# A filter's spectra from folded time rows: 34 DFT blocks in place of 58, a rounded two-pass filter product, and the token projections dealt out among the rounds

## The reference

```python
def hyena_filter_spectra(L, w_in, w_hid, b, freq, w_out):      # L = 1024
    t = jnp.linspace(0.0, 1.0, L)[:, None]
    ...
    for k, w in enumerate((w_in, w_hid[0], w_hid[1])):          # hidden width 64
        hdn = jnp.sin(freq[k] * (hdn @ w + b[k]))
    h = (hdn @ w_out).reshape(L, HY_ORDER, 2, HY_WIDTH)         # (1024, 2, 2, 1024)
    h = h * jnp.exp(-t * deltas)[:, None, None, :]
    hf, hb = h[:, :, 0], h[:, :, 1]
    k_circ = jnp.concatenate([hf[:1] + hb[:1], hf[1:], jnp.zeros_like(hf[:1]), hb[:0:-1]], axis=0)
    return jnp.fft.rfft(k_circ, axis=0)                         # length 2048
```

```python
def rms_norm(x, g):
    return (x * lax.rsqrt(jnp.mean(jnp.square(x), axis=-1, keepdims=True) + EPS) * g)
```

## Time and profile before

| | before |
|---|---|
| time, median of 3 runs | 3007.36 us (3007.21 to 3008.28) |
| span of the profiled execution | 3007.8 us |
| PE busy over the span | 2735.8 us (91%) |
| DVE busy | 1814.4 us (60%) |
| ACT busy | 919.7 us (31%) |
| POOL busy | 864.6 us (29%) |

### The profile page before, as it was taken

The page is one execution under the profiler, slowest core; times in us unless marked ns, Lnnn a source line. Parts: engine busy times, 40 slices in busy tenths (PEclk is TensorE's granted clock), DMA queues, the critical chain, the costliest instruction groups (busy, mean ns, idle before and its releaser), DMA issues. The chain is left out here.

```text
span 3007.8 us, 30927 instructions
## 1 busy us (share of the span) xinstructions
PE 2735.8 (91%) x11377; PEld 1868.0 (62%) x11377; DVE 1814.4 (60%) x2979; ACT 919.7 (31%) x1668; POOL 864.6 (29%) x635
## 2 busy tenths in 40 slices
PE   7999989978679978789999999996999997999967
PEld 3544444547546556577787899985778885444456
DVE  6255229999577658765841555553774424888553
ACT  2111121100334332536434566553432220111132
POOL 0000000005022137576633233325642221343235
PEclk9999999989889989999999999998999998999979
DMA  4211411110100034244756323314421123111043
GB/s 152 81 70 60 144 65 42 31 47 1 57 1 1 1 147 153 65 147 159 272 177 212 94 46 92 75 31 150 137 85 42 49 72 142 60 60 60 28 172 108
DMA packets 109562, 269.80 MB, mean 90 GB/s; under 512 B 18464, under 2 KB 34664, under 8 KB 105001
## 3 DMA queue, kind: packets, MB, share of 16 engines
q1 hardware_dynamic: 109418, 267.90, 26.7%
HBM read 206.87 MB, written 60.99 MB: 89 GB/s over the span
## 5 line engine op out<-in xcount | busy, mean ns | idle before, releaser
L313 PE MATMUL psum<-part,part 128*128 128x512 f32 (+1 forms) x1984 | 766.8, 386 | 78.0 <-POOL part L1604 28.1
L314 PE MATMUL psum<-part,part 128*128 128x512 f32 (+1 forms) x1984 | 743.2, 375 | 0.0
L315 PE MATMUL psum<-part,part 128*128 128x512 f32 (+1 forms) x1984 | 741.6, 374 | 0.0
L1604 POOL TENSOR_TENSOR part<-arena,part 128x512 fp32r<-128x512 f32 (+1 forms) x298 | 426.0, 1440 | 633.0 <-ACT part L1598 632.7
L313 PEld LDWEIGHTS psum<-part,part 128*128 128x128 f32 x1984 | 379.2, 191 | 163.8 <-POOL part L1604 68.5
L314 PEld LDWEIGHTS psum<-part,part 128*128 128x128 f32 x1984 | 380.2, 192 | 70.9 <-issue 3.2
L315 PEld LDWEIGHTS psum<-part,part 128*128 128x128 f32 x1984 | 378.8, 191 | 72.4
L1598 ACT ACTIVATE part<-arena 128x512 fp32r<-128x512 f32 (+1 forms) x298 | 181.6, 620 | 364.8 <-PE psum L315 237.5
L221 PE MATMUL psum<-arena 128*128 128x512 f32 (+1 forms) x672 | 232.3, 505 | 17.4 <-DMA arena<-in_w_f 9.7
L1135 POOL TENSOR_TENSOR arena<-arena 128x256 f32<-128x256 f32 x56 | 39.1, 700 | 704.7 <-PE psum L1148 704.7
L766 PE MATMUL psum<-arena 128*128 128x512 f32 x464 | 200.6, 593 | 0.7 <-issue 0.7
(11 more groups left out here) (311 smaller groups left out, 4003.8 us busy)
## 6 DMA issues: line engine op xcount, KB each, us to landing
arena<-in_ada_w SPq DMA_DIRECT2D x24, 1024.0 KB, 5.5
arena<-in_w_hy SPq DMA_DIRECT2D x40, 512.0 KB, 3.3
scratch_spec<-arena SPq DMA_DIRECT2D x68, 256.0 KB, 2.0
arena<-scratch_spec SPq DMA_DIRECT2D x12, 1024.0 KB, 5.1
arena<-in_w_gate SPq DMA_DIRECT2D x16, 512.0 KB, 3.9
arena<-in_w_out SPq DMA_DIRECT2D x16, 512.0 KB, 3.8
arena<-in_w_mgate SPq DMA_DIRECT2D x16, 512.0 KB, 3.7
arena<-in_w_mout SPq DMA_DIRECT2D x16, 512.0 KB, 4.2
```

Source lines behind the costliest of these rows:

```text
L313: nc.tensor.matmul(acc, a_hi, b_hi, start=start, stop=False)
L314: nc.tensor.matmul(acc, a_hi, b_lo, start=False, stop=False)
L315: return nc.tensor.matmul(acc, a_lo, b_hi, start=False, stop=stop)
L1604: self.K.nc.gpsimd.tensor_tensor(self.lo[s][:, c], self.raw[s][:, c], self.hi[s][:, c].bitcast(F32), ALU.subtract).then_inc(self.split, 1)
```

## The change

Every stage but the first has the same instructions as before. In `stage_spectra_tokens`:

- **Time order.** The host lays the 1024 times out as 512 early ones and, beside each t, its mirror 1024 - t. `fold_even` adds and subtracts the two halves (two operations of 2048 elements), so that every block of frequencies needs 128 rows of cosine and 128 of sine: two matmuls for each, 34 in a pair of s, 136 in all. `fold_odd` does the turns for the odd residues. Both work on `ed` and `Y`, of which there is now one each, not one for each s.
- **Product.** The hidden output and the output weights are split into a rounded part and a rest. `hid` has 128 rows: the rounded part in rows 0 to 63, the rest in 64 to 127 (layer 2 of the hidden layers is computed twice, in both halves of the rows). The product is two matmuls on rounded operands (L820 and L821 in the kernel after) for each tile. DVE takes two tiles at a time out of PSUM.
- **Order.** Eight rounds k, one for each half, order and s. Each has an even part (residues 0, 4, 2 and 6, with 10 matmuls for s = 0 and 8 for s = 1) and an odd part (8 matmuls). The products of round k + 1 stand before and between the two parts of round k, the tokens of one tile at the start of rounds 0 to 6 and of one more in the middle of rounds 0 and 1. ACT computes the decay for 512 channels at a time. Two PSUM banks serve the blocks, not four, and one each the latents and the values, not two.
- **Transfers.** The tokens are loaded in three pieces of columns straight to where the next stage wants them; before, they were loaded in this stage and again at its end (L555).

```diff
 def spec_blocks(n, comp):
-    size = lambda m: len(RES_TILES[min(PAIRS[m], 8 - PAIRS[m])])
...
+    at = 2 if comp == 2 else NSPEC0 + 2 * n if comp == 1 else 2 * n + 2 if n else 0
+    return [(at + q, y) for q, y in enumerate(SPEC_SLOTS[PAIRS[n]])]
-def radix(K, dve, link, x, Y, tmp, ready):
...
+def fold_even(K, dve, link, x, sums, Y, s, ready):
+    v = K.nc.vector
+    early, late = x[:, 0:4, :], x[:, 4:8, :]
+    v.tensor_tensor(sums, early, late, ALU.add)
+    link(v.tensor_tensor(early, early, late, ALU.subtract))
+    even, odd = (sums, early) if s == 0 else (early, sums)
+    v.tensor_tensor(Y[:, 0:2, :], even[:, 2:4, :], even[:, 0:2, :], ALU.add)
+    link(v.tensor_tensor(Y[:, 2:4, :], even[:, 2:4, :], even[:, 0:2, :], ALU.subtract))
+    dve.sem_inc(ready, 1)
+    if s == 0:
+        v.tensor_copy(even[0:1, 2, :], odd[0:1, 2, :])
+        link(v.tensor_tensor(odd[0:1, 2, :], odd[0:1, 2, :], x[0:1, 6, :], ALU.add))
+    ends, turned = even[:, 0:4:2, :], Y[:, 1:4:2, :]
+    v.scalar_tensor_tensor(out=Y[:, 4:6, :], in0=turned, scalar=C8, in1=ends, op0=ALU.mult, op1=ALU.add)
+    link(v.scalar_tensor_tensor(out=Y[:, 6:8, :], in0=turned, scalar=-C8, in1=ends, op0=ALU.mult, op1=ALU.add))
+    dve.sem_inc(ready, 1)
+    return odd
+def fold_odd(K, dve, link, x, odd, Y, s, ready):
...
+    if s == 1:
+        link(K.nc.vector.tensor_copy(Y[0:1, 12:16, :], x[0:1, 6, :].unsqueeze(1).broadcast_to((1, 4, HALF))))
...
@@ vector @@
             make_weights()
...
+            rest_of_weights(0)
+            for j in range(2):
+                cols = slice(j * HALF, (j + 1) * HALF)
+                dve.wait_ge(hid_rounded, j + 1)
+                v.tensor_tensor(hid[64:128, cols], h_raw[64:128, cols], hid[64:128, cols].bitcast(F32), ALU.subtract)\
+                    .then_inc(hid_split, 1)
+            for k, (o, h, s) in enumerate(ORDER):
+                dve.wait_ge(decay_ready, h + 1)
+                for q in range(4):
...
+                    v.tensor_tensor(ed[:, 2 * q:2 * q + 2, :], acc, decay[:, 2 * q:2 * q + 2, :], ALU.mult)\
+                        .then_inc(hd_ev, 1)
+                if k - 1 in AT_MIDDLE:
+                    take_latent(AT_MIDDLE[k - 1])
+                if k == 0:
+                    sum_weights(1)
+                    rest_of_weights(1)
+                if k == 7:
+                    norm_latents()
...
+                if k:
+                    dve.wait_ge(sp_mm, done[k - 1][0])
+                odd = fold_even(K, dve, link, ed, sums, Y, s, y_ready)
+                if k in AT_START:
+                    take_latent(AT_START[k])
+                if k:
+                    dve.wait_ge(sp_mm, done[k - 1][1])
+                fold_odd(K, dve, link, ed, odd, Y, s, y_ready)
@@ scalar @@
+                if k == 7:
+                    act.wait_ge(meansq, 1)
+                    a(rstd[:, 1:9], rstd[:, 1:9], ACT.Sqrt)
@@ tensor @@
+            def hidden_out(k, q):
...
+                if n >= 2:
+                    pe.wait_ge(hd_ev, n - 1)
+                pe.wait_ge(w_split, h + 1)
+                for e in range(2):
+                    acc, c = K.bank(2 * (n % 2) + e), slice((2 * q + e) * P, (2 * q + e + 1) * P)
+                    mm(acc, hid[:, c], w_hi[h][:, o, s, :], start=True, stop=False)
+                    last = mm(acc, hid[0:64, c], w_lo[h][0:64, o, s, :], start=False, stop=True)
...
+            for k in range(8):
+                if k in AT_START:
+                    token_products(AT_START[k])
+                if k < 7:
+                    hidden_out(k + 1, 0)
+                    hidden_out(k + 1, 1)
...
+                for n, p, comp in groups_of(k, 0):
+                    group(k, n, p, comp)
+                if k < 7:
+                    hidden_out(k + 1, 2)
+                    hidden_out(k + 1, 3)
+                else:
+                    turn_latents()
+                if k in AT_MIDDLE:
+                    token_products(AT_MIDDLE[k])
+                for n, p, comp in groups_of(k, 1):
+                    group(k, n, p, comp)
```

526 lines of the change are left out of this document (268 added, 258 removed).

## The result

The kernel after takes 2974.22 us (median of 4 runs, 2972.20 to 2974.85), the kernel before in the same comparison 3007.61 us (3007.21 to 3008.28). The ratio is 0.9889, with a 95% interval of 0.9877 to 0.9901: 33 us or 1.1% faster. Forecast were 2946.4 us and a range of 2930 to 2970: the direction was right, the size too large by 28 us.

What follows compares the result with a forecast made beforehand. PE was taken to bound the first stage. Start 43.9, rounds 34.4 + 37.7 + 36.5 + 113.8 + 40.7 gave 307.0 us, with 5 of clock 312.0 against 372.96: 61 us less, 2946.4 us, range 2930 to 2970.

Steps and rivals of the forecast that it cites:

- What bounds the kernel: First stage up to its barrier: PE's work sets the length; later stages, with the same instructions, were costed at nothing.
- the prices: Unit costs read from the earlier trace: block matmul 0.86 us, rounded matmul 0.23 us, two-tile product 0.93 us, plus DVE operations.
- the loop: Rounds 3 to 6, fold_odd to fold_odd through PE and DVE: 27.8 us for s = 0, 29.1 for s = 1, together 113.8.
- the sum: Start and eight rounds added up to the end of the first stage's last block: 307.0 us before any clock loss.
- The start: Hidden layers and first products: first tile out of PSUM at 43.9 us against 43.03 before, costing 1 us.
- The folds, the copy, the way out of PSUM: DVE costs per round: fold_even 9.5 or 10.7 us, fold_odd 8.9 or 10.1, copy 1.25, four PSUM operations 1.2 each.
- The latent's waits: DVE waits for PE before the latent: 2 to 4 us in rounds 3 to 6, 3 to 7 us per tile in rounds 1 and 2.
- The clock: PE's idle gaps in the first stage lower its clock, an allowance of 5 us in all.
- a sign of error: A mean granted clock below 0.9 in the first stage would show the forecast wrong.
- the second rival: Clock falls in every round, needing gaps over 2 us in rounds 3, 4 and 6: 24 us lost, 2965 us; chance 0.17.
- Costlier operations on DVE: Rival: PSUM operations, the copy and strided fold writes at upper bounds cost some 20 us, 2966 us; chance 0.04.
- From span to time: Whole program: the median time was taken to lie 0.4 us below the profiled span, 2946.4 us from 2946.8.

Runs made afterwards that it cites:

- Experiment 1: The kernel after with full rows: the second matmul of each product takes all 128 rows, adding the product of the rests; 2948.16 us, ratio 0.9799.
- Experiment 2: The kernel after with product matmuls grouped by rows: for two tiles, both 128-row matmuls, then both 64-row ones; 2964.21 us, ratio 0.9856.
- experiment 5: The kernel after with full 128-row products, and the load of the decay rates issued ahead of the small parameters; 2948.18 us, ratio 0.9796.
- experiment 7: The kernel after with full 128-row products, and the latent taken out of PSUM behind fold_odd, not between the folds; 2940.57 us, ratio 0.9771.
- experiment 6: The kernel after with full 128-row products, and six unread stand-in matmuls in PE's wait at the end of round 0; 2947.66 us, ratio 0.9800.
- experiment 8: The kernel after with full 128-row products, tile 0's tokens ahead of the first products, later tiles one place earlier; 2946.93 us, ratio 0.9803.
- experiment 3: The kernel after with a plain float32 product, one 64-row matmul per tile, without rounding, rests or doubled rows; 2964.47 us, ratio 0.9856.
- experiment 4: The kernel after with unread stand-in matmuls: 12 behind the hidden layers, 6 at the end of round 0; 2971.85 us, ratio 0.9882.

## Why the prediction was wrong, point by point

**What bounds the kernel** was right: up to the barrier PE's work sets the length, and what lies behind changed by 1.8 us.

**The step that failed** is in the prices: "On rounded operands a matmul takes 0.23 us, a product of two tiles (four matmuls) 0.93 us." The rows were of matmuls that all load 128 rows, and the change's product loads 128 and 64 rows in turn. It measured 1.72 us. The mechanism was right and the size of this term off by 0.79 us for each of 32 products, 25 us of PE's time. Experiment 1 removes the alternation with the same number of matmuls, and the last block comes to 313.94 us, 19.6 of the 21.6 us that the stage was over. Experiment 2, which halves the number of changes, halves the surcharge of a product. The trace before has no such pair, but it has changes of rows, between the products (L736, 64 rows) and the blocks (L766, 128 rows):

```profile
136.14 7.13 PE L736 MATMUL psum<-arena 64*128 64x512 f32 x16
143.20 14.00 PE L766 MATMUL psum<-arena 128*128 128x512 f32 x32
157.13 14.00 PE L736 MATMUL psum<-arena 64*128 64x512 f32 x32
```

16 records 0.43 us apart are 6.88 us, but the blocks start after 7.06 us; 32 are 13.76 us, but the products start after 13.93 us. Just under 0.2 us a change could be read there, as the remainder of a group, and 0.93 us with four such changes is 1.7 us. At the least the price should have been bounded from both sides: 0.93 us from the earlier trace rows, and 1.72 us from a matmul every 0.43 us, the float32 pace in the same rows. The upper bound, 25 us more on PE, would have put the forecast's upper end beyond 2970 us.

The term acted in two places. Between the first operation out of PSUM and the odd part the loop passes two products (4.71 us against 3.4 in the sum); and PE's pile in a round grew by 3.2 us, from 28 to 31 us for s = 0 and from 26 to 29 us for s = 1, so that PE, and no longer the loop, was the limit: rounds 3 to 6 took 123.6 us, forecast 113.8, with full rows 116.9.

**The start** was short by 2.7 us: DVE ended the hidden layers at 37.98 us, not at 36.0, and the first product took 3.1 us at half clock, not 1.9; the chain of rounding and rests between them took 5.55 us, not 6.0. There the sum had a misreading: the 1171 ns of the earlier trace rows are the mean of two forms, 1024 elements alone took 1064 ns, and the rounding of 2048 took 1.89 us in the kernel after, where 2.3 and 2.4 stand in the sum. "ACT's decay comes before its first sine (about 0.7 us...)" took the decay for mostly done; it had waited until 8.29 us for the load of its rates, and the first sine came at 15.90. Full rows took 0.6 us off the first tile's time and the earlier load (experiment 5) another 2.3 us, to 43.68 us, forecast 43.9.

**The folds, the copy, the way out of PSUM** held: the copy of 2048 elements took 1.22 us (forecast 1.25), the four operations out of PSUM 1.22 us each (1.2), round 7 with full rows 40.76 us (40.7), the wait for the root 8.0 us (7). Round 0 with full rows was 1.5 us shorter than the sum.

**The loop.** The latent's waits with full rows were 8.4 us in three rounds, 2 to 4 us each as forecast, and experiment 7 shows that they lay on the loop.

**The clock** was allotted 5 us. The granted clock was 0.96 as a mean over the stage in the change, not below the 0.9 that was to be a sign of error. In the change more time was lost by it (round 1 was 6.6 us over, and six stand-ins took 5 us off it, though rounds 2 and 5 lost as much). With full rows and the earlier decay the eight rounds and the start come to 312.55 us against 307.0: all 5.5 us that were left are of the size of the allotment. That they are all clock was not shown: filling one gap gave back 1 us, and rounds 4 and 6 were 1.3 and 1.6 us over with windows at 0.94, while round 4 took 28.01 us in experiment 6, at a granted clock of 1.00 from 180 to 210 us. Nor did the clock need the gaps of over 2 us that the second rival asked for: in the change it fell in round 5 with PE busy throughout, just after a product,

```profile
253.00:256.50 3.50, 3.50 (x5) 1.34 (x5) 3.47 (x5) 0.00 (x0) 0.00 (x0) 0.55 0.00 0
```

which cost some 1.6 us (3.5 us at 0.55).

**The rivals.** Costlier operations on DVE (2966 us) and a clock that falls in every round (2965 us) were nearest in size, and neither was the cause: DVE's operations had their prices, and the clock was 1.00 in the windows of rounds 3 to 6 but for one at 0.94. What was missing among them is a rival on the price of the product.

**From span to time.** The profiled execution's time was 2.0 us above its span here, not below it, and the runs spread by 2.7 us. What follows the stage has the same instructions in all these kernels and took from 2631.2 us (experiment 8) to 2639.1 us (experiment 7). Differences of 4 us in the time are therefore no evidence on the stage, whose last block in the profile is the finer measure. It is the measure of one execution each, though, and holds what the clock did in it, 2 to 4 us in experiments 2 and 3; of gains below that (experiments 4 to 6, 8) only those of single rounds are firm. Of the 26, 10 and 10 us that experiments 1 to 3 took off the time, the stage accounts for 19.6, 4.4 and 2.2, and the rest of the program, which took 2636.6 us in the change and 2632.1 to 2633.8 in these three, for 2.8, 3.3 and 4.5. The last 3.5, 2.3 and 2.9 us come from which execution was profiled: in the change one 2.0 us below the median, in these three one 0.3 to 1.5 us above. Why the rest varies stays open: no kernel was made for that.

## What to carry to other kernels

A matmul's price belongs to its surroundings: before a pace is taken from a trace, look whether its neighbours load weights for the same number of rows as yours will, and whether a group that follows one with other rows takes longer than its records; and if a pair would alternate, fill up the rows (here they even held useful data) or group the matmuls by rows. When two engines take turns in a loop, look for the operation that waits for a third thing in the middle of it, and put it where its engine is early anyway. A serial tail, such as a root and norms ahead of the last round, belongs into a round that has room.

## What the runs showed of the hardware

- **A change of rows between matmuls costs 0.20 us at full clock.** Rounded matmuls of 512 columns start 0.23 us apart when they all use 128 rows, and 0.43 us when 128 and 64 rows alternate; the weight load then starts with its own matmul. At half clock the two are 0.43 and 0.72 us. The surcharge is the length of one load, 0.18 to 0.19 us and 0.29 us. Between groups of float32 matmuls it is 0.17 to 0.19 us, in both directions (experiment 3 and the kernel before). The load itself is as long for 64 rows as for 128 (0.18 and 0.19 us). The Trainium skill (TensorE: Matmul & The Clock Gate, What happens when you issue a matmul) states that a load goes ahead of running matmuls where the row groups don't conflict or where it targets the background buffer, and that its time goes by the columns. On the columns the trace agrees. On the first point, loads into the very rows that are in use went ahead in experiment 1, which fits the second case, and those that changed the number of rows did not.
- **Some dense work left the clock down.** In experiment 4, 24 matmul records on 33 rows and 64 columns ran at the pace of half clock to the end of their 20.7 us, without a gap between them, and the products after them did too. In the change the 16 product matmuls from 43.53 us to 55.10 us, every second one on 64 rows, kept that pace as well, and it rose behind the first token products (128 rows), after 57.66 us. In experiment 1, where the products on 128 rows began after the same gap of 13.6 us, the first eight were 0.43 us apart and those from 47.38 us on 0.23.
- **The clock's falls don't go by the gaps alone.** At the end of round 0 a gap of 5.61 us in the change had some 12 us of work at half clock behind it. With full rows, 2.76 us had some 3 us (experiment 1), 4.02 us had some 6 us (experiment 5), and 2.66 us none (experiment 8, granted clock 1.00 from 80 to 100 us). In round 5 of the change it fell without any gap, and in round 3 the same wait of PE for ACT (2.3 us, until 183 us) had a fall behind it in experiment 1 and none in experiment 6.
